# Prompt attention on one Trainium2 core: the inverted softmax sums transposed once and spread through memory, the value products in two PSUM banks by turns

## The reference, cut to what matters

```python
s = jnp.einsum('bqhd,bkhd->bhqk', qb, kf) * scale + (cb[..., :, None] - ck_h[..., None, :])
s = jnp.where(k_pos[None, :] <= q_pos[:, None], s, -jnp.inf)
p = jax.nn.softmax(s, axis=-1)
return jnp.einsum('bhqk,bkhd->bqhd', p, vf)
```

## Time and profile before

| | |
|---|---|
| median of 3 runs | 1360.45 us (1357.02 to 1362.4) |
| the profiled execution's own time | 1364.08 us |
| its span | 1362.1 us |
| granted PE clock, mean of the span | 0.95 |
| prompt attention's loop | from 202.5 to about 276 us of the span |
| the samples' attention | to about 367 us |

### The profile page before, as it was taken

One profiled execution on the slowest core, in us unless ns is written; L12 is line 12 of the kernel. 1 busy time (PEld: TensorE's weight loads), 2 busy tenths in 40 slices (PEclk: granted clock), 3 DMA queues, 4 the chain that ended last, 5 costly groups with the idle time before them and its releaser, 6 DMA issues.

```text
span 1362.1 us, 16370 instructions
## 1 busy us (share of the span) xinstructions
PE 1204.9 (88%) x6249; PEld 633.4 (47%) x6249; DVE 404.4 (30%) x856; ACT 253.9 (19%) x600; POOL 250.2 (18%) x284
## 2 busy tenths in 40 slices
PE   7999999998899899778878999998899899877880
PEld 6755675566545433233325754445744533333330
DVE  6742116644303521111126201113611612111115
ACT  2111117733203010000013100014412101000001
POOL 2351404322000111111010000304810011111102
PEclk8999999999899899888989999998999899889995
DMA  8321308599876599999956140402357689999966
GB/s 297 105 70 71 132 2 287 185 341 366 309 309 262 200 412 420 421 420 420 412 203 204 63 128 0 139 0 87 109 167 316 243 325 420 420 420 420 419 250 216
DMA packets 104511, 340.25 MB, mean 250 GB/s; under 512 B 22478, under 2 KB 40850, under 8 KB 80618
## 3 DMA queue, kind: packets, MB, share of 16 engines
q1 hardware_dynamic: 89800, 303.24, 58.5%
q0 software_dynamic: 14336, 35.80, 7.3%
q10 hardware_dynamic: 290, 0.08, 0.0%
HBM read 322.45 MB, written 31.31 MB: 260 GB/s over the span
## 4 chain that ended last, share of the span: by engine, by line
PE 58%; SPq 14%; DMA 12%; DVE 7%; POOL 3%; issue 2%; ACT 1%; PEldq 1%; PEld 0%; POOLq 0%; DVEq 0%; ACTq 0%
SPq L1355 10%; PE ps L1565 9%; PE ps L2071 8%; DMA moe_gu<-in_moe_w_up 7%; PE ps L613 6%; PE ps L1490 6%; PE ps L2022 4%; SPq L1377 4%; PE ps L1583 4%; PE ps L609 4%; DMA fox_arena<-negs_rows 3%; PE ps L957 2%; PE ps L969 2%; PE ps L980 2%; DMA moe_gu<-expert_rows 1%
## 5 line engine op out<-in xcount | busy, mean ns | idle before, releaser
L1565 PE MATMUL ps<-moe_gu,rows 128*64 128x512 f32 x1024 | 245.5, 635 | 55.6 <-DMA moe_gu<-in_moe_w_up 52.3
L1565 PEld LDWEIGHTS ps<-moe_gu,rows 128*64 128x64 f32 x1024 | 81.0, 146 | 199.8 <-issue 192.3
L1852 DVE TENSOR_TENSOR turned<-turned,ps 128x256 f32<-128x256 f32 x32 | 13.5, 421 | 305.1 <-ACT turned L1668 305.1
L1449 POOL DMA_INDIRECT expert_rows<-turned,moe_row x32 | 32.1, 1002 | 392.0 <-ACT turned L1678 359.9
L1583 PE MATMUL ps<-moe_wd,moe_rowsel 128*64 128x512 f32 x352 | 80.4, 598 | 1.9 <-DVE turned L1857 1.9
L1668 ACT ACTIVATE turned<-ps 128x256 f32<-128x256 f32 x32 | 12.3, 384 | 302.8 <-PE ps L1565 302.8
L2071 PE MATMUL ps<-mwblk,turned 128*128 128x512 f32 x128 | 56.0, 594 | 1.5 <-DVE vaug L2290 1.5
L448 POOL TENSOR_TENSOR fox_arena<-fox_arena 128x512 f32<-128x512 f32 x32 | 44.6, 1416 | 64.9 <-PE ps L609 55.2
L2071 PE MATMUL ps<-m_arena,turned 128*128 128x512 f32 x128 | 55.7, 593 | 0.7 <-ACT m_arena L2175 0.7
L613 PE MATMUL ps<-x,fox_arena 128*128 128x288 f32 x224 | 56.0, 406 | 0.0
L2022 PE MATMUL ps<-turned,mwblk 128*128 128x288 f32 x224 | 54.6, 406 | 0.0
(11 more groups left out here) (386 smaller groups left out, 1735.0 us busy)
## 6 DMA issues: line engine op xcount, KB each, us to landing
moe_gu<-in_moe_w_gate SPq DMA_DIRECT2D x56, 1024.0 KB, 21.8
moe_gu<-in_moe_w_up SPq DMA_DIRECT2D x56, 1024.0 KB, 24.1
moe_wd<-in_moe_w_down SPq DMA_DIRECT2D x44, 1024.0 KB, 24.1
rows<-in_moe_w_down SPq DMA_DIRECT2D x20, 1024.0 KB, 22.6
fox_arena<-in_cache_v POOLq DMA_DIRECT2D x32, 512.0 KB, 12.6
fox_arena<-in_fox_w_in SPq DMA_DIRECT2D x6, 2048.0 KB, 10.1
fox_arena<-in_cache_k SPq DMA_DIRECT2D x20, 512.0 KB, 9.9
moe_gu<-in_moe_w_gate SPq DMA_DIRECT2D x16, 512.0 KB, 10.1
```

The source lines that it names most:

```text
L1565: mm = pe.matmul(ps[h, 2 + p % 2, :].rearrange("s (k f) -> s k f", k=2), xT[:, c, h], gu[s][:, half, :, c, :], start=(c == 0), stop=(c == ...
```

## The change

PE no longer spreads the sums. One transpose of the pair's 8 columns (`turn_sums`) puts them as 8 rows of 128 into a free corner of bank 5, behind the transposes of the next pair's first step. DVE copies the 8 rows to a small tile (`keep_sums`). SP writes the 4 KB tile to DRAM, waits for it, and reads it back with two broadcasts, one per head, to 64 partitions each, 256 KB in all (`spread_rows`). DVE's `output` waits for these reads. ACT's copy of bank 7 is gone, and bank 7 serves the value products of every other pair, so that `values` waits for the `output` two pairs back. `spread_rows(p - 2)` stands in SP's list behind the loads of pair p; `spread_rows(6)` behind all of them; `spread_rows(7)` behind `keys_in(2)`. The first scores of the samples on PE also wait for the last `keep_sums`.

```diff
+        rinv_dram = nc.dram_tensor("rinv_rows", (PAIRS, 2 * (NT - 1), P), F32, kind="Internal").ap()
...
+            rb_rows = sb("pa_rb", [2 * QT_, P], where=pa)
...
+                def spread_rows(p):
+                    sp.wait_ge(rb_kept, p + 1)
+                    sp.dma_start(rinv_dram[p], rb_rows[:]).then_inc(rb_out, 16)
+                    sp.wait_ge(rb_out, 16 * (p + 1))
+                    if p:
+                        sp.wait_ge(o_kept, p)
+                    for h in range(2):
+                        sp.dma_start(spread[h * FD:(h + 1) * FD, :].rearrange("d (t q) -> d t q", q=P),
+                                     rinv_dram[p].rearrange("(t h) q -> h t q", h=2)[h:h + 1].broadcast_to([FD, QT_, P])
+                                     ).then_inc(rb_in, 16)
...
+                    spread_rows(p - 2)
+                spread_rows(PAIRS - 2)
...
                 keys_in(2)
+                spread_rows(PAIRS - 1)
...
+                    if t == 0 and h and s:
+                        mm = turn_sums(pe, s // QT_ - 1)
                     mm.then_inc(t_done, 1)
...
-                    if p:
-                        pe.wait_ge(o_kept, p)
+                    if p >= 2:
+                        pe.wait_ge(o_kept, p - 1)
                 for h in range(2):
-                    mm = pe.matmul(ps[h * FD:(h + 1) * FD, 6, k * P:PROMPT], ...
+                    mm = pe.matmul(ps[h * FD:(h + 1) * FD, 6 + p % 2, k * P:PROMPT], ...
...
-            def spread_sums(pe, p):
+            def turn_sums(pe, p):
                 pe.wait_ge(inverted, p + 1)
-                for t in range(QT_):
-                    for h in range(2):
-                        n = 2 * (QT_ * p + t) + h
-                        mm = pe.matmul(ps[h * FD:(h + 1) * FD, 7, t * P:(t + 1) * P], rinv[:, n:n + 1].broadcast_to([P, FD]),
-                                       ident, start=True, stop=True)
-                mm.then_inc(rb_done, 1)
+                return pe.transpose(ps[0:2 * QT_, 5, 3 * P:4 * P], rinv[:, 2 * QT_ * p:2 * QT_ * (p + 1)], ident)
...
+                    pe.wait_ge(rb_kept, PAIRS)
...
-                        spread_sums(pe, PAIRS - 1)
+                        pe.wait_ge(t_kept[1], STEPS)
+                        turn_sums(pe, PAIRS - 1).then_inc(rb_done, 1)
...
-                        if k == 2:
-                            spread_sums(pe, p)
...
+            def keep_sums(dve, p):
+                if p:
+                    dve.wait_ge(rb_out, 16 * p)
+                dve.tensor_copy(rb_rows[:], ps[0:2 * QT_, 5, 3 * P:4 * P]).then_inc(rb_kept, 1)
...
                 if h:
+                    if t == 0 and s:
+                        keep_sums(eng, s // QT_ - 1)
                     eng.tensor_copy(dst, src).then_inc(t_kept[1], 1)
...
-                def keep_spread(p):
-                    act.wait_ge(rb_done, p + 1)
-                    if p:
-                        act.wait_ge(o_kept, p)
-                    act.activation(spread, ps[:, 7, :], ACT.Copy).then_inc(rb_kept, 1)
...
-                    if s >= 8 and s % QT_ == 0:
-                        keep_spread((s - 8) // QT_)
...
-                    dve.wait_ge(rb_kept, p + 1)
+                    dve.wait_ge(rb_in, 32 * (p + 1))
                     dve.wait_ge(pv_done, QT_ * (p + 1))
-                    dve.tensor_tensor(turned[:, p, 0:PROMPT], ps[:, 6, :], spread, ALU.mult).then_inc(o_kept, 1)
+                    dve.tensor_tensor(turned[:, p, 0:PROMPT], ps[:, 6 + p % 2, :], spread, ALU.mult).then_inc(o_kept, 1)
...
+                dve.wait_ge(rb_done, 1)
+                keep_sums(dve, PAIRS - 1)
                 output(PAIRS - 1)
```

More of the change, by code:

```diff
@@ L840, in fox_attention @@
                                                             sem("pa_rb_kept"), sem("pa_o_kept"))
+            rb_out, rb_in = sem("pa_rb_out"), sem("pa_rb_in")
             dec_in, dec_own = sem("dec_in"), sem("dec_own")
@@ L976, in values @@
                         pe.wait_ge(t_kept[h], QT_ * (p + 1))
-                    if p:
-                        pe.wait_ge(o_kept, p)
+                    if p >= 2:
+                        pe.wait_ge(o_kept, p - 1)
                 for h in range(2):
-                    mm = pe.matmul(ps[h * FD:(h + 1) * FD, 6, k * P:PROMPT], v[:, k, (2 * p + h) * FD:(2 * p + h + 1) * FD],
+                    mm = pe.matmul(ps[h * FD:(h + 1) * FD, 6 + p % 2, k * P:PROMPT], v[:, k, (2 * p + h) * FD:(2 * p + h + 1) * FD],
                                    pT[:, h, k, k * P:PROMPT], start=(k == 0), stop=(k == QT_ - 1))
                 mm.then_inc(pv_done, 1)
-            def spread_sums(pe, p):
+            def turn_sums(pe, p):
                 pe.wait_ge(inverted, p + 1)
-                for t in range(QT_):
-                    for h in range(2):
-                        n = 2 * (QT_ * p + t) + h
-                        mm = pe.matmul(ps[h * FD:(h + 1) * FD, 7, t * P:(t + 1) * P], rinv[:, n:n + 1].broadcast_to([P, FD]),
-                                       ident, start=True, stop=True)
-                mm.then_inc(rb_done, 1)
+                return pe.transpose(ps[0:2 * QT_, 5, 3 * P:4 * P], rinv[:, 2 * QT_ * p:2 * QT_ * (p + 1)], ident)
             def d_turn_keys(pe, b, pairs):
@@ L1135, in act_ @@
                         keep_turned(act, s - 2, 0)
-                    if s >= 8 and s % QT_ == 0:
-                        keep_spread((s - 8) // QT_)
                     if s < STEPS:
                         soft(s)
-                keep_spread(PAIRS - 1)
                 def d_keep_keys(b, p):
```

## The result

The changed kernel takes 1390.81 us (median of 4 executions, 1388.62 to 1397.25) against 1361.41 before (4 executions): ratio 1.0226, 95% interval 1.0187 to 1.0265, or 29 us more. The forecast was 15 us more. Its own profiled execution took 1388.93 us with a span of 1387.5.

The account below looks back on a forecast made before the run. PE was taken to bound the loop, the DMA engines the samples' stage. 3.0 + 5.2 + 0.3 + 6.9 = +15 us made 1379.5 us profiled, 1375.5 on the median, with PE's 6.3 inside the periods; range 1361 to 1402.

Parts of the forecast that it names:

- The first pair: Start of the loop: the first pair's output comes at 222.5 instead of 219.45 us, +3.0 us.
- The late bias rows: SP's bias rows go behind the reads, some 8 us later, and cost nothing while a landing stays below 8 us.
- The room of 4.9 us: Time between DVE's sums' copy and its output: 5.84 us, less 0.9 once PE is faster; the trip wouldn't fit.
- Where between: Step sizing the loop's five periods from output(0) to output(5) by SP's queue emptying: 52.1 against 46.9 us, +5.2.
- The end: From the last pair's first copy to output(7): 19 against 12.1 us, +6.9, passed on in full through a DMA gap.
- The 0.3 for the sums' copy once more: Term for DVE's added copy of the sums, counted once more before the last pair's first copy: +0.3 us.
- Net 0.9 us ... if PE stays the bound: PE's saving per pair in the loop, for 7 pairs 6.3 us, already inside the forecast periods.
- The hidden case: Rival: write and reads land within the 4.9 us before DVE's output, PE's 6.3 us are gained, 1353.6 us; 8%.
- The clock: PE's granted clock in the loop: forecast above 0.9; rival 0.79 through pauses, 5 us more, 1380.5 us, 8%.
- the forecast's 10.4: Loop periods expected from output(0) to output(5): 10.1, 11.7, 11.7, 9.3 and 9.3 us; the forecast had 55%.
- the fully loaded rival: Rival: every DMA landing stays at the loop's median, trip 13.4 us, period 16.9, time about 1421 us; 12%.
- the quiet 5.7: Least trip through memory on quiet DMA engines: 1.6 + 0.4 + 3.5 us, and 0.2 for handovers.

## Why the prediction came out half

**Right.** The direction, and the mechanism in outline: the trip is longer than its room, DVE's order puts the wait into every pair, and the last trip opens a gap on the DMA engines that reaches the experts, all but 2.3 us of it. The first pair: +3.0 foreseen, +2.3 measured. The late bias rows cost nothing, as foreseen. The room of 4.9 us for a trip of at least 5.7; the quietest was 7.7, the mean 9.4. Behind the loop SP and POOL's page loads moved with output(7), and the DMA share fell to 0.39 behind it. DVE's added copy took 0.28 us.

**Wrong: the step "Where between".** It let the queue in front of the write empty at the full 328 GB/s from 2 us on, 10.0, 11.6, 11.6, 9.2 and 9.2 us behind the reads' issue, and so had periods of 9.3 to 11.7. Measured from reads to next reads: 14.2, 12.8, 15.1, 13.7 and 13.3. That is 21.9 us in five periods where the sum had 5.2, and all other terms together are right to 1.1 us. By parts of the five periods: the writes took 25.5 us up to the next issue, where the sum had 14.4; from the reads' issue to the output it was 24.5 instead of 20.0; from the output to the write's issue 18.8 instead of 17.7. The last of them by stretches of 2 us, from its reads' issue at 272.80 (columns as above):

```profile
272.80:274.80 2.00, 1.67 (x16) 1.28 (x16) 0.42 (x5) 1.96 (x8) 0.00 (x0) 1.00 0.15 45
274.80:276.80 2.00, 0.92 (x5) 0.18 (x3) 0.18 (x1) 0.01 (x1) 0.00 (x0) 1.00 0.49 142
276.80:278.80 2.00, 0.75 (x4) 0.34 (x6) 1.86 (x7) 0.45 (x2) 0.49 (x1) 1.00 0.75 152
278.80:280.80 2.00, 2.00 (x8) 0.30 (x4) 1.23 (x5) 1.16 (x6) 0.96 (x2) 0.71 1.00 174
280.80:282.80 2.00, 2.00 (x7) 0.41 (x6) 0.20 (x2) 1.06 (x4) 0.45 (x1) 0.50 0.95 300
282.80:284.80 2.00, 2.00 (x15) 1.33 (x16) 1.26 (x4) 0.58 (x2) 0.39 (x2) 0.93 1.00 290
```

The first two microseconds, in which almost nothing moves, are the ones that the step had. What it hadn't is the six behind them, in which the sums and the first bias rows move at 142 to 174 GB/s. Only then comes a rate near the one that I had taken. Over the five cycles, from 216.95 to 286.06 us, it was 208 GB/s at a share of 0.70; the step's own bytes over its own times are 262. In the earlier trace rows share and rate come from a stretch in which SP never waited for a landing. Dividing by the share made of them a full rate that the burst behind the reads doesn't reach at first: in the fourth stretch above the share is 1.00 and the rate 174. Why bias rows issued back to back moved so slowly, no run tells. Nor was free DMA time as scarce as the prediction says: 256 KB more per pair cost nothing.

The step did treat reads, rows, pages and write as one cycle, and counted no cost for what SP doesn't issue while it stands in its wait. The kernel before with an unused trip (+20 us) shows that this can cost as much by itself, by bias rows that come late; in the changed kernel those rows were late too, but DVE was held by the sums before it could be held by them.

**The end: the size right, the places not.** 6.9 foreseen. To output(7) it was 9.1, and the samples' stage behind it was 2.3 us shorter than I passed on, so from the last pair's first copy to the experts it is 6.8. Some luck is in that: the gap behind output(7) was there, but nothing had told me of the 2.3. The 0.3 for the sums' copy once more didn't show. The last trip by itself is some 4.7 of it.

**Mis-sized, the gain.** "Net 0.9 us ... if PE stays the bound" is 0.4 us. PE's busy 9.38 of 9.38 hid that the copies' chain was 0.4 us behind it. The hidden case would have been some 1360, an estimate, and no gain that can be told. The figures of the Trainium skill behind its 5.0 us ("DMA: Bandwidth & Descriptors", "Anatomy of one DMA — SWDGE (gpsimd) path") are for transfers that GpSimd issues; here SP issued both, and the quietest trip took 7.7 us.

**The clock.** Foreseen above 0.9 in the forecast, 0.79 as a rival: it was 0.88 over the five periods and 0.50, the lower of its two levels (1.2 GHz), in the worst stretch shown; PE had been busy for 1.67 of the 4 us from 274.80, and the clock fell in the stretches behind. From the output to the next sums' copy it then took 4.1 us instead of 3.0 in two of the five, so some 2 us in all, inside the 21.9.

The five periods, 13.8 us in the mean, lie half-way between the forecast's 10.4 and the fully loaded rival's 16.9; the trips, 9.4 us in the mean of all eight, lie half-way between its 13.4 and the quiet 5.7. The range held the time.

## What to carry to other kernels

A blocking wait for a DMA on the queue that feeds the machine can cost in two ways: whoever needs the data waits, and the loads behind it aren't issued. Here either was enough to keep the pair at 12.6 us or above, and only the version without both came near the old period. So take them out together before judging either. Size the cycle of such a queue (issue, backlog, landing, next issue) by rates read from a queue that starts from empty, not from one that never runs dry. And before trading work of a busy engine against a transfer, take the transfer out altogether for one run: here it would have shown that the prize was about 2 us of 1361.

## What I had not expected of the hardware

A 4 KB write to memory took 1.2 us to the next issue with nothing issued in front, and 2.9 to 6.9 us in the changed kernel's loop; on a queue of its own, 3.8 to 5.8 us, it was hardly earlier. In the one write looked at in detail, 16 packets on ACT's queue first moved 3.8 us or more after their issue, while SP's and POOL's queues drained. The Trainium skill, "DMA: Bandwidth & Descriptors", section "Queues, rings and completion order", has each engine take turns between its queues packet by packet; by that the write would have been early. The measurement decides: it was late, though the trace doesn't show at which point it was held.
